# Two-block transformer layer on one core: squares of x moved from ScalarE to GpSimd, and products of four weight units put in k-tile order

## What is computed

```python
def rms_norm(x, g):
    xf = x.astype(jnp.float32)
    y = xf * lax.rsqrt(jnp.mean(xf * xf, axis=-1, keepdims=True) + NORM_EPS)
    return (y * g.astype(jnp.float32)).astype(x.dtype)
...
        h = rms_norm(x, pre_mix_g[l])
        z = h @ w_in[l]
```

## Time and profile before

| what | value |
| --- | --- |
| median of 3 runs | 2158.75 us (2156.2 to 2159.53) |
| profiled execution, its own time | 2157.67 us |
| span of that execution in the trace | 2155.8 us |
| PE busy | 2125.0 us, 99% of the span |
| DVE busy | 1466.6 us, 68% |
| ACT busy | 1064.3 us, 49% |
| POOL busy | 85.8 us, 4% |

### The profile page before, as it was taken

One profiled execution on the slowest core, in us unless ns is written; L12 is line 12 of the kernel. 1 busy time (PEld: TensorE's weight loads), 2 busy tenths in 40 slices (PEclk: granted clock), 3 DMA queues, 4 the chain that ended last, 5 costly groups with the idle time before them and its releaser, 6 DMA issues.

```text
span 2155.8 us, 36129 instructions
## 1 busy us (share of the span) xinstructions
PE 2125.0 (99%) x13982; PEld 1805.2 (84%) x13982; DVE 1466.6 (68%) x2084; ACT 1064.3 (49%) x1521; POOL 85.8 (4%) x75
## 2 busy tenths in 40 slices
PE   9999999999999999999999999999999999999998
PEld 7888888888888888888788888887788888888886
DVE  6656578885578855885894699874776544567656
ACT  6444464444444433444644867544434544456543
POOL 0800000000000000000000000001311000000000
PEclk9999999999999999999999999999999999999999
DMA  9655556665666556655565666653454655644553
GB/s 308 210 158 163 169 167 185 187 192 183 199 189 190 186 185 203 187 177 180 163 218 163 184 178 179 211 157 83 128 177 132 193 179 193 193 150 147 175 196 117
DMA packets 398872, 384.43 MB, mean 178 GB/s; under 512 B 43676, under 2 KB 395476, under 8 KB 397780
## 3 DMA queue, kind: packets, MB, share of 16 engines
q1 hardware_dynamic: 397672, 381.61, 56.7%
q10 hardware_dynamic: 1072, 1.05, 0.2%
HBM read 375.73 MB, written 6.87 MB: 177 GB/s over the span
## 4 chain that ended last, share of the span: by engine, by line
PE 89%; DVE 7%; issue 1%; ACT 1%; DMA 1%; SPq 0%; POOL 0%; DVEq 0%; ACTq 0%
PE acc L900 35%; PE acc L903 17%; PE acc L1026 5%; PE acc L1028 5%; PE acc L1027 5%; PE acc L937 2%; PE aux L1370 2%; PE acc L992 2%; PE acc L994 2%; PE acc L993 2%; DVE w_lo L3075 1%; PE acc L1670 1%; PE acc L1671 1%; PE acc L1672 1%; PE acc L940 1%
## 5 line engine op out<-in xcount | busy, mean ns | idle before, releaser
L2513 DVE TENSOR_TENSOR w_lo<-raw_w,w_hi 128x1024 fp32r<-128x1024 f32 (+1 forms) x568 | 681.0, 1224 | 434.0 <-ACT w_hi L1743 433.2
L1743 ACT ACTIVATE w_hi<-raw_w 128x1024 fp32r<-128x1024 f32 (+1 forms) x568 | 584.0, 1045 | 701.2 <-PE acc L903 412.9
L900 PE MATMUL acc<-h,w_hi 128*128 128x512 f32 x1664 | 525.7, 397 | 0.0
L903 PEld LDWEIGHTS acc<-h,w_lo 128*128 128x128 f32 x1664 | 312.6, 188 | 73.8
L903 PE MATMUL acc<-h,w_lo 128*128 128x256 f32 x1664 | 327.0, 278 | 0.0
L900 PEld LDWEIGHTS acc<-h,w_hi 128*128 128x128 f32 x1664 | 254.6, 189 | 1.0
L900 PE MATMUL acc<-x_split,w_hi 128*128 128x512 f32 x704 | 225.1, 401 | 0.0
L900 PE MATMUL acc<-xs_b,w_hi 128*128 128x512 f32 x512 | 162.1, 398 | 2.0 <-DVE w_lo L3075 2.0
L903 PEld LDWEIGHTS acc<-x_split,w_lo 128*128 128x128 f32 x704 | 132.2, 188 | 31.2
L3075 DVE TENSOR_TENSOR w_lo<-raw_w,w_hi 128x1024 fp32r<-128x1024 f32 x96 | 116.8, 1219 | 41.6 <-ACT w_hi L2230 40.7
L900 PE MATMUL acc<-xs_a,w_hi 128*128 128x512 f32 x448 | 142.3, 399 | 0.7 <-DVE w_lo L3075 0.7
(11 more groups left out here) (462 smaller groups left out, 3216.6 us busy)
## 6 DMA issues: line engine op xcount, KB each, us to landing
raw_w<-in_w_up SPq DMA_DIRECT2D x172, 512.0 KB, 3.6
raw_w<-in_a_w_in SPq DMA_DIRECT2D x124, 512.0 KB, 4.2
raw_w<-in_w_in SPq DMA_DIRECT2D x64, 512.0 KB, 4.1
raw_w<-in_w_down SPq DMA_DIRECT2D x64, 512.0 KB, 3.8
raw_w<-in_b_w_qg SPq DMA_DIRECT2D x64, 512.0 KB, 3.7
raw_w<-in_w_o SPq DMA_DIRECT2D x32, 512.0 KB, 3.8
raw_w<-in_a_w_out SPq DMA_DIRECT2D x32, 512.0 KB, 3.7
raw_w<-in_w_k_shared SPq DMA_DIRECT2D x32, 512.0 KB, 4.7
```

The lines of the kernel that those rows point to most:

```text
L900: pe.matmul(ACC[2 * b + f], WHI[:, q if hi is None else hi, k, f * P:(f + 1) * P], op[:, kt, :, :].rearrange("p h t -> p (h t)"), start=fi ...
L903: mm = pe.matmul(ACC[2 * b + f][:, 0:T], WLO[:, slot, k, f * P:(f + 1) * P], op[:, kt, 0, :], start=False, stop=last)
L1743: act.activation(WHI[:, u % 4, 0:ku, :], RAWW[:, u, 0:ku, :], ACT.Copy).then_inc(hi_made, 1)
L2513: dve.tensor_tensor(WLO[:, u, 0:ku, :], RAWW[:, u, 0:ku, :], WHI[:, u % 4, 0:ku, :].bitcast(F32), ALU.subtract)\
```

## The change

GpSimd makes the four squares, each 128 x 1024, as one `tensor_tensor` of four tiles by themselves. It takes each quarter as soon as its tiles have landed. ACT makes none. PE's products of units 4 to 7 wait for the unit's rest at once and then go by k-tile over all four tiles; in units 2 and 3 the second half goes by k-tile as well, the first half as before.

```diff
+            pool.wait_ge(first_x, 16)
+            for j in range(4):
+                x4 = X[:, 4 * j:4 * j + 4, :]
+                pool.wait_ge(x_in[j], 16)
+                pool.tensor_tensor(SQ1[:, 4 * j:4 * j + 4, :], x4, x4, ALU.mult).then_inc(sq_ready, 1)
+
             pool.wait_ge(z_ready, 4)
...
+            def both_parts(u, ks):
+
+                x, b = u // 2, u % 2
+                for k in ks:
+                    for f in range(2):
+                        pe.matmul(ACC[2 * b + f], WHI[:, u % 4, k, f * P:(f + 1) * P], A1[:, KU * x + k, :, :].rearrange("p h t -> p (h t)"),
+                                  start=False, stop=False)
+                    for f in range(2):
+                        mm = pe.matmul(ACC[2 * b + f][:, 0:T], WLO[:, u, k, f * P:(f + 1) * P], A1[:, KU * x + k, 0, :],
+                                       start=False, stop=(x + k == 6))
+                return mm
...
-                    pe.wait_ge(hi_made, u + 1)
-                    half_hi(u, 0)
-                    pe.wait_ge(lo_made, seen(lo_made))
-                    half_rest(u, 0)
-                    half_hi(u, 1)
-                    half_rest(u, 1).then_inc(unit_done, 1)
+                    if u < 4:
+                        pe.wait_ge(hi_made, u + 1)
+                        half_hi(u, 0)
+                        pe.wait_ge(lo_made, seen(lo_made))
+                        half_rest(u, 0)
+                        both_parts(u, (2, 3)).then_inc(unit_done, 1)
+                    else:
+                        pe.wait_ge(lo_made, seen(lo_made))
+                        both_parts(u, range(KU)).then_inc(unit_done, 1)
...
-            def square1(j):
-                act.activation(SQ1[:, 4 * j:4 * j + 4, :], X[:, 4 * j:4 * j + 4, :], ACT.Square).then_inc(sq_ready, 1)
-
...
                 split_unit(2 * j)
-                if j == 3:
-                    act.wait_ge(x_in[0], 16)
-                    square1(0)
                 split_unit(2 * j + 1)
-            for j in range(1, 4):
-                square1(j)
```

## The result

| | median, us | runs |
| --- | --- | --- |
| before | 2157.24 (2154.62 to 2159.53) | 22 |
| changed | 2160.38 (2158.56 to 2162.76) | 22 |

The ratio is 1.0016, 95% interval 1.0010 to 1.0022: slower by 3.1 us of the medians (by the interval 2.2 to 4.7), inside the 0.2% that I called no change, and clear of zero only because there were so many runs. The profiled span is 2158.5 us, 2.7 more than before.

What follows compares the result with a forecast made beforehand. PE was taken as the bound, waiting early for operands from DVE. Holds of 6.92 us less idle 1.88 and 0.64, slack and small savings cost 3.3 us: 2158.75 + 3.3 = 2162.1 us, range 2158.4 to 2165.0.

Steps and rivals of the forecast that it cites:

- rival 3: At the start, squares miss DVE's path: one hold fewer gives 1.6 us, none -0.26; 2158.5 to 2160.4 us, chance 0.12.
- the base: Whole kernel: the time before the change, taken as 2158.75 us, to which the forecast added 3.3 us.
- GpSimd's reading holds DVE: During the squares, DVE instructions reading two SBUF tensors are blocked while GpSimd reads SBUF; four holds, 6.92 us.
- A waiting GpSimd goes first: At the squares, a waiting GpSimd gets its turn when DVE's instruction ends, ahead of DVE's next.
- A hold of 1.73 us: Each square, 1.91 us long on GpSimd, was to delay DVE by 1.73 us, the first 0.18 us not felt.
- The dearer hold of 2.2 us: Rival at the squares: each holds DVE 2.2 us, costing 5.2 us, time 2164 us; chance 0.22.
- Idle time of 1.88 and 0.64 us is used up first, then 0.86 us of slack at unit 4: Before unit 4, DVE's idle time cuts 6.92 us of holds to 4.40; PE's slack then leaves about 3.6.
- The order's wait: At unit 4, PE waits for the unit's rest before its first product: some 0.9 us of the delay.
- 0.21 us saved at the squares' products: After unit 5, PE's wait for ACT's last square was to vanish, saving 0.21 us.
- 0.05 us by the order: In the first units' products, going by k-tile instead of in halves was to save PE 0.05 us.
- ScalarE's relief: At the start, the 3.9 us of squares taken off ACT were to count for nothing, nothing on the path being behind them.
- the fallen clock: Rival at the start: PE's granted clock falls to half from 13 us on, costing 4.2 us, time 2163; chance 0.15.

Runs made afterwards that it cites:

- two_quarters: The changed kernel with GpSimd squaring only quarters 0 and 1 and ScalarE the others; median 1.1 us above the kernel before, ratio 1.0005.
- two_tensors: The changed kernel with GpSimd adding a tensor of ones to each quarter instead of squaring it; median 4.7 us above the kernel before, ratio 1.0025.
- placed: The changed kernel with the squares of quarters 2 and 3 waiting until DVE has made unit 5's rest; median 1.5 us above the kernel before, ratio 1.0005.
- squares_only: The changed kernel with the products in the old order, squares still on GpSimd; median 2.5 us above the kernel before, ratio 1.0013.
- writes_only: The kernel before with the new product order and four GpSimd memsets at the quarters' landings, squares on ScalarE; median 0.0 us from before, ratio 1.0000.

## Why the prediction was right, point by point

- *The result.* 3.3 us were forecast, 3.1 measured, 2.99 at the landmark. The terms that were off partly cancelled: 0.6 us too much for the holds, 0.26 too much taken off. The measured 2160.38 lies below the 2161 to 2163.2 that I named as the forecast itself, and inside the 2158.5 to 2160.4 of rival 3. The number alone could not tell them apart; the traces do, with all four squares in DVE's path. It is the base, 1.5 us too high, that moved the number.
- *GpSimd's reading holds DVE.* Shown: by the four lengthened rows, by their absence with memsets, and by eight holds in place of four.
- *A waiting GpSimd goes first.* Right for the four squares of the changed kernel, but not always: in two_quarters (11.02) and in two_tensors (the second subtraction behind 18.01) DVE had one more instruction. Why is open.
- *A hold of 1.73 us.* Mis-sized: 1.58 (mean of 1.64, 1.44, 1.63, 1.63). The row's own length was right, 1.90 against 1.91, but 0.3 us of it, not 0.18, pass beside DVE, and 0.2 of them at its end: the tiles at 19.10 are done at 22.40 and take 1.67 us, so DVE went on at 20.73, and GpSimd's row ends at 20.93. Four times 0.15 is 0.6 us too much. The dearer hold of 2.2 us is wrong for a square; the holds of 2.1 us of two_tensors lie near it. The Trainium skill ("GPSIMD Engine Reference", section 3.1) gives 2.6 cycles an element, an estimate of 2.2 us for 1024; the square's 1.90 us are less and the 2.46 us of the sum of two tensors more.
- *Idle time of 1.88 and 0.64 us is used up first, then 0.86 us of slack at unit 4.* Right in the changed kernel: 3.74 us of DVE's delay gave 3.00 at unit 4 (3.74 - 0.86, and 0.11 from the end of the rest to the load, where I had 0.05). It was too simple for fewer squares. PE also waits for tiles 2 and 3 and for unit 2's rest, where there is no slack; placed lost 0.8 us there, ahead of unit 4.
- *The order's wait costs 0.9 us once DVE is late.* Right: 0.85 in the trace, 0.84 between the changed kernel and squares_only, and nothing alone.
- *0.21 us saved at the squares' products.* Wrong. From unit 5's start to the squares' load are 2.98 us in the changed kernel (26.45 to 29.43) and 3.01 before (23.45 to 26.46), though GpSimd's last square is done 8 us ahead. The gap belongs to the change of products, not to a wait. *0.05 us by the order*: not seen. From unit 4's first load to the landmark are 13.67 us against 13.68. So 0.26 us that I took off were never there.
- *ScalarE's relief counts for nothing.* Right: no row of PE answers to it. Where PE is some 0.3 us earlier, as in writes_only, ScalarE's last square (26.04) is just what its products wait for, so little was missing.
- *Rivals.* The dearer hold was shown with other operands and the fallen clock with twice the squares; neither happened in the changed kernel. The squares that miss DVE's path can be had by placing them.

## What to carry to other kernels

Before moving work to GpSimd, look at what DVE reads at that moment. If DVE's instructions take two SBUF inputs, GpSimd's reading time is taken from DVE's time, and the question is DVE's slack, not GpSimd's. With one such input they aren't held. In the kernel before, while GpSimd multiplies two SBUF tensors from 1485.06 to 1487.42, DVE runs these (`aux` lies in PSUM, where PE writes its results, and not in SBUF):

```profile
1485.98 0.42 DVE L3131 TENSOR_TENSOR wkv_x<-aux,wkv_x 128x256 f32<-128x256 f32 x1 [1.21 <-PE aux L1370]
1486.56 0.42 DVE L3134 TENSOR_SCALAR head_rstd_rows<-aux 128x256 f32<-128x256 f32 x1 [0.15 <-PE aux L1474]
1487.18 0.43 DVE L3137 COPY wkv_small<-aux 64x256 f32<-64x256 f32 x1 [0.20 <-PE aux L1370]
```

They are no longer than the same lines with GpSimd idle: lines 3131 and 3137 take 0.43 us at 1492.29 and 1493.40.

Landing order is a poor moment then; behind a point where DVE is ahead of its consumers the same work was free. A wait that costs nothing today (the rest of a unit ahead of its first product) has a price that shows only when its producer becomes late.

## What the runs showed of the hardware

- GpSimd's time depends on its inputs: 1.90 us for 128 x 1024 with both inputs one tensor, 2.36 for a product of two tensors. In the same place, the first row of the start, it was 2.01 with one tensor and 2.46 with two. For DVE the difference was 1.58 against 2.1 us.
- DVE goes on some 0.2 us before GpSimd's row ends (20.73 and 20.93). GpSimd, once waiting, mostly gets the turn at the end of DVE's current instruction; in two traces DVE had one more. A head start of DVE's row doesn't decide it: in placed DVE's row starts at 6.16 and GpSimd's at 6.19, and DVE was held all the same (that tile took 2.20 us, and the next one 0.47); in two_quarters DVE's instruction began 0.30 us behind GpSimd's row and was not held.
- A DVE instruction with one SBUF input ran beside a reading GpSimd at its usual length (0.42 us at 1485.98), one with two waited.
